# A state space mixer in chunks of 128 tokens with carried states, its preparation spread between the tiles of a branch projection

## The reference

```
c, L = s // CHUNK, CHUNK                                  # 4 chunks of 128 tokens
a_cs = jnp.cumsum(a, axis=2)                              # a = dt * A, within the chunk
decay = jnp.exp(jnp.where(causal, a_cs[l] - a_cs[s], -inf))
cb = jnp.einsum('bclgn,bcsgn->bclsg', cm, bm)
y_diag = jnp.einsum('bclsgr,bcsgrp->bclgrp', cb[..., None] * decay, xdt)
chunk_states = jnp.einsum('bclgn,bclgr,bclgrp->bcgrpn', bm, jnp.exp(a_cs[:, :, -1:] - a_cs), xdt)
state = state * chunk_decay + chunk_state                 # scan over the chunks, s_prev = state before
y_off = jnp.einsum('bclgn,bcgrpn,bclgr->bclgrp', cm, s_prev, jnp.exp(a_cs))
y = y_diag + y_off + xs * d_skip;  y = rmsnorm(y * silu(z))
```

## Time and profile before

| | |
|---|---|
| median of three runs (us) | 3278.84 |
| lowest and highest (us) | 3278.44, 3281.72 |
| span of the profiled execution (us) | 3281.5 |
| own time of the profiled execution (us), the run that goes with this span | 3281.72 |
| PE busy, share of the span | 97% |
| PEld, DVE, ACT, POOL busy | 77%, 56%, 28%, 11% |
| mean granted TensorE clock | 0.980 |

### The profile page before, as it was taken

The page is one execution under the profiler, slowest core; times in us unless marked ns, Lnnn a source line. Parts: engine busy times, 40 slices in busy tenths (PEclk is TensorE's granted clock), DMA queues, the critical chain, the costliest instruction groups (busy, mean ns, idle before and its releaser), DMA issues.

```text
span 3281.5 us, 37188 instructions
## 1 busy us (share of the span) xinstructions
PE 3186.0 (97%) x13833; PEld 2526.1 (77%) x13833; DVE 1850.9 (56%) x2389; ACT 923.5 (28%) x1243; POOL 346.3 (11%) x160
## 2 busy tenths in 40 slices
PE   8989999999999999999998999999999999999999
PEld 6767567877788887888877788887888887588887
DVE  8796435437776655554476755445454446465432
ACT  2443233323222222222222322222222234322222
POOL 2334014022000000000023000002000031000000
PEclk9999889999999999999999999999999998999999
DMA  3222002321323222223332222232223321022232
GB/s 129 78 77 90 26 32 90 116 77 61 119 91 99 96 97 91 90 96 99 102 107 77 77 96 96 97 103 95 96 96 99 105 76 46 7 97 90 96 105 88
DMA packets 79372, 287.67 MB, mean 88 GB/s; under 512 B 9056, under 2 KB 9312, under 8 KB 78880
## 3 DMA queue, kind: packets, MB, share of 16 engines
q1 hardware_dynamic: 77328, 278.03, 25.7%
q0 software_dynamic: 1936, 8.13, 0.7%
HBM read 284.02 MB, written 2.10 MB: 87 GB/s over the span
## 4 chain that ended last, share of the span: by engine, by line
PE 76%; issue 14%; POOL 5%; DVE 4%; ACT 1%; DMA 0%; POOLq 0%; DVEq 0%; ACTq 0%
PE ps L589 23%; PE ps L591 23%; PE ps L590 23%; POOL w_lo L543 5%; PE ps L682 1%; PE ps L1066 1%; PE ps L698 1%; PE ps L927 1%; PE ps L748 0%; PE ps L1065 0%; PE ps L1072 0%; DVE rstd L1566 0%; ACT w_hi L1110 0%; DVE w_lo L1502 0%; PE ps L933 0%
## 5 line engine op out<-in xcount | busy, mean ns | idle before, releaser
L589 PE MATMUL ps<-h_hi,w_hi 128*128 128x512 f32 (+1 forms) x2443 | 966.9, 396 | 33.8 <-POOL w_lo L543 20.8
L590 PE MATMUL ps<-h_lo,w_hi 128*128 128x512 f32 (+1 forms) x2443 | 956.4, 391 | 0.0
L591 PE MATMUL ps<-h_hi,w_lo 128*128 128x512 f32 (+1 forms) x2443 | 955.4, 391 | 0.0
L1110 ACT ACTIVATE w_hi<-raw 128x1024 fp32r<-128x1024 f32 x525 | 555.4, 1058 | 1315.6 <-PE ps L591 1297.8
L1502 DVE TENSOR_TENSOR w_lo<-raw,w_hi 128x1024 fp32r<-128x1024 f32 x390 | 476.9, 1223 | 450.3 <-ACT w_hi L1110 449.8
L589 PEld LDWEIGHTS ps<-h_hi,w_hi 128*128 128x128 f32 x2443 | 464.2, 190 | 142.8 <-POOL w_lo L543 24.6
L591 PEld LDWEIGHTS ps<-h_hi,w_lo 128*128 128x128 f32 x2443 | 464.0, 190 | 97.0
L590 PEld LDWEIGHTS ps<-h_lo,w_hi 128*128 128x128 f32 x2443 | 464.0, 190 | 96.5 <-issue 2.4
L589 PE MATMUL ps<-mid_hi,w_hi 128*128 128x512 f32 x1208 | 477.7, 395 | 2.0 <-DVE mid_lo L1577 2.0
L591 PE MATMUL ps<-mid_hi,w_lo 128*128 128x512 f32 x1208 | 476.9, 395 | 0.0
L590 PE MATMUL ps<-mid_lo,w_hi 128*128 128x512 f32 x1208 | 476.8, 395 | 0.0
(11 more groups left out here) (363 smaller groups left out, 2687.4 us busy)
## 6 DMA issues: line engine op xcount, KB each, us to landing
raw<-in_wstream SPq DMA_DIRECT2D x525, 512.0 KB, 3.3
x<-in_x SPq DMA_DIRECT2D x8, 256.0 KB, 5.6
x_in<-in_x POOLq DMA_DIRECT2D x8, 256.0 KB, 3.0
mem_x<-in_mem POOLq DMA_DIRECT2D x2, 1024.0 KB, 5.2
out<-x POOLq DMA_DIRECT2D x8, 256.0 KB, 3.5
tmp<-in_ret_decay POOLq DMA_DIRECT2D x1, 1024.0 KB, 5.2
rope_r<-in_rope_r POOLq DMA_DIRECT2D x1, 512.0 KB, 3.7
mats<-in_mats SPq DMA_DIRECT2D x1, 320.0 KB, 6.6
```

The costliest lines, as they stand in the source:

```text
L589: nc.tensor.matmul(dst, hi_w, hi_x, start=first, stop=False)
L590: nc.tensor.matmul(dst, hi_w, lo_x, start=False, stop=False)
L591: return nc.tensor.matmul(dst, lo_w, hi_x, start=False, stop=last)
L1110: nc.scalar.activation(w_hi[:, n % HL], raw[:, r], ACT.Copy).then_inc(hi_ready, 1)
```

## The change

It makes the mixer work as the reference does, chunk by chunk:

- A head has one `spread` over 512 columns (two matmuls, one bank, banks 4 and 5 by turns) and no mask by matmul. ACT takes the fall within the chunk with four `Relu` of 128 columns and then one `Exp` of 512; `cb` is now only the four diagonal blocks, multiplied by a 0/1 triangle in the preparation; DVE masks a head with one product of 512 (`masked`); PE makes four blocks of 128 columns (`y_diag`). `decay` has four slots in place of two.
- Six `chunk_state` matmuls of 512 columns, DVE's `weigh` and `carry`, and for each pair `y_carried` (three matmuls of 128 columns into bank 6) make the part that comes from earlier chunks. ACT makes `grown`, the exponential of the running sums (64 rows by 384 a head, two slots for pairs), and DVE's `pair_in` has three instructions in place of one.
- dt is multiplied into `xs_tok` when it is drained (four products of 128 columns in place of one copy for each of 8 tiles), no longer into `decay`.
- The preparation stands between the tiles of `br1`; the four scans (128 columns each, on 16 rows) stand ahead of the first product of `br1` on DVE; two of the eight gate tiles stand between the transposes of x, the other six one a pair in the loop.

```diff
+            br1_tiles(0, 2)
...
+            br1_tiles(2, 4)
...
+            br1_tiles(4, 6)
+            pe.wait_ge(aux_used, turned)
+            nc.tensor.matmul(aux_tile()[:, 0:64], IDENT[:, P - 1:P].to_broadcast([P, P]), acs_tok, start=True, stop=True)\
+                .then_inc(aux_done, 1)
+            br1_tiles(6, 8)
...
+            xs_turned(0, 4)
+            gate_tile(0)
+            xs_turned(4, 8)
+            gate_tile(1)
             pe.wait_ge(aux_used, aux[0])
+            pe.wait_ge(acs_ready, 2)
...
             def spread(hd):
+                if hd >= 2:
+                    pe.wait_ge(grown_done, hd - 1)
                 sel = ident_r[0:16, hd:hd + 1].to_broadcast([16, P])
-                for j, (b, cs) in enumerate(BANK_CHUNKS):
-                    if hd:
-                        pe.wait_ge(decay_done, 3 * hd - 2 + j)
-                    lo, hi = OFF[cs[0]], OFF[cs[-1]] + WIDTH[cs[-1]]
-                    dst = ps[:, b, 0:hi - lo]
-                    nc.tensor.matmul(dst, sel, acs_hi[:, lo:hi], start=True, stop=False)
-                    nc.tensor.matmul(dst, sel, acs_lo[:, lo:hi], start=False, stop=True)
-                    for c in cs:
-                        o = OFF[c] - lo
-                        mm = nc.tensor.matmul(dst[:, o:o + P], ident_r[:], neg_r[:, 0], start=False, stop=True,
-                                              skip_group_check=True)
-                mm.then_inc(bcast_done, 1)
-            spread(0)
-            for hd in range(SSD_HEADS):
-                if hd + 1 < SSD_HEADS:
-                    spread(hd + 1)
-                p = hd // 2
-                t, rows = st.t + 2 * p, slice(SSD_P * (hd % 2), SSD_P * (hd % 2) + SSD_P)
+                dst = ps[:, 4 + hd % 2]
+                nc.tensor.matmul(dst, sel, acs_hi[:], start=True, stop=False)
+                nc.tensor.matmul(dst, sel, acs_lo[:], start=False, stop=True).then_inc(bcast_done, 1)
+            def y_diag(hd):
+                t, rows, feats = y_tile(hd // 2), slice(SSD_P * (hd % 2), SSD_P * (hd % 2) + SSD_P), slice(SSD_P * hd, SSD_P * hd + SSD_P)
                 if hd % 2 == 0:
                     bank_free(t)
-                else:
-                    tile_part(st.n + p, t + 1, h_hi, h_lo, 0, 1, KB)
                 pe.wait_ge(m_ready, hd + 1)
                 for c in range(CH):
-                    mm = nc.tensor.matmul(bank(t)[rows, P * c:S], xs_tok[:, c, SSD_P * hd:SSD_P * hd + SSD_P],
-                                          decay[:, hd % 2, OFF[c]:OFF[c] + WIDTH[c]], start=c == 0, stop=True,
-                                          skip_group_check=c > 0)
+                    mm = nc.tensor.matmul(bank(t)[rows, P * c:P * c + P], xs_tok[:, c, feats],
+                                          decay[:, hd % 4, P * c:P * c + P], start=True, stop=True)
                 mm.then_inc(y_done, 1)
+            def chunk_state(g, c, b):
+                k = (CH - 1) * g + c
+                pe.wait_ge(weighed, g + 1)
+                if k >= 2:
+                    pe.wait_ge(state_taken, k - 1 if g == 0 else k)
+                nc.tensor.matmul(ps[:, b], b_tok[:, g, c], xw_tok[:, c, S * g:S * g + S], start=True, stop=True)\
+                    .then_inc(state_done, 1)
+            def y_carried(p):
+                g = p // 4
+                pe.wait_ge(state_taken, (CH - 1) * (g + 1))
+                if p:
+                    pe.wait_ge(posted, st.s + p)
+                for c in range(1, CH):
+                    mm = nc.tensor.matmul(ps[:, 6, P * c:P * c + P], states[c - 1][g][:, P * (p % 4):P * (p % 4) + P],
+                                          xbc[:, 10 + g, P * c:P * c + P], start=True, stop=True)
+                mm.then_inc(carried, 1)
+            spread(0)
+            spread(1)
+            chunk_state(0, 0, 6)
+            chunk_state(0, 1, 7)
+            for p in range(DT):
+                if p + 1 < DT:
+                    spread(2 * p + 2)
+                y_diag(2 * p)
+                if p == 0:
+                    chunk_state(0, 2, 6)
+                if p + 2 < DT:
+                    gate_tile(p + 2)
+                if p + 1 < DT:
+                    spread(2 * p + 3)
+                y_diag(2 * p + 1)
+                if 1 <= p <= 3:
+                    chunk_state(1, p - 1, 7)
+                if p:
+                    y_carried(p - 1)
+            y_carried(DT - 1)
...
+            gate_out(0)
+            split(st.n + 2)
+            gate_out(1)
             for hd in range(SSD_HEADS):
                 act.wait_ge(bcast_done, hd + 1)
-                if hd >= 2:
-                    act.wait_ge(y_done, hd - 1)
-                for b, cs in BANK_CHUNKS:
-                    for c in cs:
-                        o = OFF[c] - OFF[cs[0]]
-                        ins = nc.scalar.activation(decay[:, hd % 2, OFF[c]:OFF[c] + WIDTH[c]], ps[:, b, o:o + WIDTH[c]],
-                                                   ACT.Exp, bias=small[:, 80 + 16 * c + hd:81 + 16 * c + hd])
-                    ins.then_inc(decay_done, 1)
-                if hd % 2:
-                    split(st.n + hd // 2 + 1)
-                elif hd:
+                if hd >= 4:
+                    act.wait_ge(y_done, hd - 3)
+                for c in range(CH):
+                    ins = nc.scalar.activation(decay[:, hd % 4, P * c:P * c + P], ps[:, 4 + hd % 2, P * c:P * c + P], ACT.Relu,
+                                               bias=acs_tok[:, 16 * c + hd:16 * c + hd + 1], scale=-1.0)
+                ins.then_inc(fall_ready, 1)
+                act.wait_ge(fall_ready, hd + 1)
+                nc.scalar.activation(decay[:, hd % 4], decay[:, hd % 4], ACT.Exp, scale=-1.0).then_inc(decay_done, 1)
+                p, rows = hd // 2, slice(SSD_P * (hd % 2), SSD_P * (hd % 2) + SSD_P)
+                if p >= 2:
+                    act.wait_ge(posted, st.s + p - 1)
+                nc.scalar.activation(grown[rows, p % 2, P:S], ps[rows, 4 + hd % 2, P:S], ACT.Exp).then_inc(grown_done, 1)
+                if hd % 2 and hd // 2 < DT - 2:
+                    split(st.n + hd // 2 + 3)
+                elif hd % 2 == 0 and hd:
                     pair_out(hd // 2 - 1)
             pair_out(SSD_HEADS // 2 - 1)
...
             def pair_in(p):
-                drained_tile(st.t + 2 * p)
-                v.scalar_tensor_tensor(out=xbc[:, p], in0=xbc[:, p], scalar=vcol("ssd_d", p), in1=stage[:, (st.s + p) % 2],
-                                       op0=ALU.mult, op1=ALU.add).then_inc(posted, 1)
-            for hd in range(SSD_HEADS):
-                dve.wait_ge(decay_done, 3 * hd + 3)
-                g = hd * SSD_GROUPS // SSD_HEADS
-                for c in range(CH):
-                    rows = slice(OFF[c], OFF[c] + WIDTH[c])
-                    ins = v.scalar_tensor_tensor(out=decay[:, hd % 2, rows], in0=decay[:, hd % 2, rows],
-                                                 scalar=small[:, 16 + 16 * c + hd:17 + 16 * c + hd], in1=cb[:, g, rows],
-                                                 op0=ALU.mult, op1=ALU.mult)
-                ins.then_inc(m_ready, 1)
-                if hd and hd % 2 == 0:
-                    pair_in(hd // 2 - 1)
-            pair_in(SSD_HEADS // 2 - 1)
+                y, late = xbc[:, p], grown[:, p % 2, P:S]
+                dve.wait_ge(carried, p + 1)
+                dve.wait_ge(grown_done, 2 * p + 2)
+                done(v.tensor_tensor(late, late, ps[:, 6, P:S], ALU.mult))
+                drained_tile(st.t + (2 + 2 * p if p < DT - 2 else DT + p))
+                done(v.scalar_tensor_tensor(out=y, in0=y, scalar=vcol("ssd_d", p), in1=stage[:, (st.s + p) % 2],
+                                            op0=ALU.mult, op1=ALU.add))
+                v.tensor_tensor(y[:, P:S], y[:, P:S], late, ALU.add).then_inc(posted, 1)
+            def masked(hd):
+                dve.wait_ge(decay_done, hd + 1)
+                v.tensor_tensor(decay[:, hd % 4], decay[:, hd % 4], cb[:, hd * SSD_GROUPS // SSD_HEADS], ALU.mult)\
+                    .then_inc(m_ready, 1)
+            weigh(0)
+            masked(0)
+            carry(0, 0, 6)
+            carry(0, 1, 7)
+            masked(1)
+            carry(0, 2, 6)
+            weigh(1)
+            for hd in range(2, SSD_HEADS):
+                masked(hd)
+                if hd % 2 == 0 and hd >= 4:
+                    if hd <= 8:
+                        carry(1, hd // 2 - 2, 7)
+                    pair_in(hd // 2 - 2)
+            pair_in(DT - 2)
+            pair_in(DT - 1)
```

More of the change, by code:

```diff
@@ L346, in build @@
         u_hi, u_lo = br_hi, br_lo
+        acs = acc[0:SSD_HEADS]
+        dt_tok, acs_tok, tail, whole_chunk = (tok[:, k] for k in range(4))
+        states = [[tmp[:, 0], tmp[:, 1]], [tmp[:, 2], tmp[:, 3]], [spare[:, 0], spare[:, 1]]]
         x_squares = [tmp[:, k] for k in range(4)] + [stage[:, k] for k in range(2)] + [acc[:], spare[:, 0]]
@@ new lines, in _, with y_tile, gate_tile, xs_turned @@
```

(48 more changed lines are left out.)

119 lines of the change are left out of this document (73 added, 46 removed).

## The result

The changed kernel takes 3252.18 us (median of 4 runs, 3249.47 to 3254.73) beside 3280.28 for the kernel before on the same chip (4 runs, 3278.44 to 3286.96): 28.1 less by the medians. The ratio of all runs is 0.9909, its 95% interval 0.9896 to 0.9922. The profiled execution took 3254.7 with a span of 3252.9, against a span of 3281.5 before: 28.6 less. The forecast was 30.3 less, and 3249.

A forecast was written before the change was run, and what follows sets the result against it. PE's list of work was taken to bound the kernel. Loop 47.8 us less, 46.3 less with the preparation, minus 16 of clock loss: 30.3 less than the profiled or median time, said as 3249; range 3235 to 3267.

The forecast's parts named there:

- Preparation: From br1's first matmul to the loop: 66.1 us on PE, 1.5 more than before, with two gate tiles done in it.
- Prices on PE: Full-clock PE times in the loop: spread 0.66, four blocks 0.92, gate tile 5.67, carried part 0.69; an iteration 9.5 us.
- The ring: PE's spread waits for `grown`, that for `posted`, `pair_in` for `carried`: five pauses of 2.8 to 3.6 us, 15.6 together.
- The end of the loop: After the last gate tile, heads 13 to 15 and the last carried parts, without cover for ACT: 16.0 us at full clock.
- One sign that was to show the forecast wrong: In the loop, PE waiting for `m_ready`, that is for ACT's Relu or Exp.
- The clock: In the loop, 2.7 us lost at each of five pauses and the end: 16, ends 0 and 32.
- The sum: Whole kernel: 46.3 less at full clock, minus 16 of clock loss, 30.3 us less.
- its sign: For the loop's start: it begins within 2 us of 346.5.
- Rival 1: In the loop, each iteration's pause keeps the clock at 1.2 GHz throughout: 69 us more, 3301; chance 5%.
- Rival 2: In the loop, no pauses, `posted` earlier or the wait hidden: 15.6 less and half the clock loss, 3225; chance 9%.
- Rival 3: In the loop, POOL's panel work slows DVE's six `pair_in` by 2.1 us each: 12.6 more, 3261; chance 18%.
- the count of the prediction: In the loop, POOL's 2.45 us starts some 4.5 us into the iteration and ends ahead of `pair_in`.

The follow-up runs named there:

- e_prep: Changed kernel with its preparation put back in single stretches: all br1 tiles first, gate tiles 0 and 1 last; 3261.75 us, ratio 0.9934 to the kernel before.
- e_both: Changed kernel with a third `grown` slot, and `y_carried` and `chunk_state` ahead of the gate tile; 3219.84 us, in another session 3216.58.
- e_slots: Changed kernel with a third slot for `grown`, so ACT waits for the result of pair p-3; 3222.59 us, ratio 0.9829 to the kernel before.
- e_early: Changed kernel with `y_carried` and `chunk_state` moved ahead of the gate tile on PE, both slots kept; 3222.06 us, ratio 0.9829 to the kernel before.
- e_fill: Changed kernel plus 11 unread 128x512 matmuls after the carried part of iterations 1 to 5; 3244.48 us, ratio 0.9896 to the kernel before.
- e_zc: Changed kernel with third `grown` slot, carried part ahead of gate tile, and z's tiles 0 and 1 inside iterations 6 and 7; 3221.66 us.

## Why the prediction was right, point by point

- **Preparation**: forecast 66.1, measured 64.7 beside 64.6 before, so 1.4 less than forecast. PE has no wait there but one of 1.73 for the first panel. The small matmuls between the tiles took 6.4, forecast 7.7 with the 0.5 for a wait that didn't come. DVE's drains of x, forecast 9, took 6.6. e_prep shows what the covers are worth.
- **Prices on PE**: `spread` and blocks came nearly as read (at full clock 380.68 to 381.33 is 0.65 and 381.33 to 382.35 is 1.02, forecast 0.66 and 0.92). The first iteration took 9.9 (forecast 9.7), that of p = 1 10.8 (10.4); e_both's 9.66 stands against 9.5. Each block of 128 columns costs a little more than a quarter of 512.
- **The ring**: place, releaser, number and size as forecast: 14.0 us against 15.6. L1945, L1947 and L1949 have means of 0.55, 0.75 without one outlier, and 0.56 against 0.58, 0.75 and 0.58. `carry` added 0.66 where 0.8 was said. Two edits that open the ring at different places, e_slots and e_early, confirm the mechanism.
- **The end of the loop**: 21.84 from the spread at 434.14 to z, forecast 16.0 and a clock share of 2.7. One collision with POOL is in it, below. What is left, 21.84 - 16.0 - 1.65 = 4.2, is the clock, if the 16.0 was right; no run measures that number at full clock without another change. One sign that was to show the forecast wrong did appear here: PE waits for a head's mask (L1953) for 4.26 us. It is the one wait of that kind that the 16.0 had counted in, for head 15, and no iteration before has it.
- **The clock**: forecast 16 for six places, 2.7 each. Against e_slots' iteration of 10.74 and e_both's 9.66 the iterations from 370.20 lost 3.2, 3.2, 3.4 and 1.9, and with the end's 4.2 that is 15.9. The sum is right and its reason was not; that is luck. The loss of before was taken over, 21 us for eight pairs. But a third of the low clock stood in a stretch that hadn't begun in the loop. The kernel before stood in its preparation for 5.22 us ahead of 339.81, the clock fell at 338.7 in that wait and stayed low until 359.2, far into the loop (columns as in the earlier trace rows):

```profile
334.60:339.80 5.20, 0.00 (x0) 0.00 (x0) 5.03 (x8) 0.00 (x0) 0.00 (x0) 0.90 0.00 0
338.80:345.00 6.20, 4.63 (x24) 4.20 (x24) 5.70 (x11) 0.00 (x0) 0.00 (x0) 0.50 0.00 0
345.00:359.20 14.20, 13.35 (x28) 6.82 (x28) 4.40 (x7) 4.51 (x9) 1.47 (x1) 0.50 0.01 1
359.20:487.30 128.10, 128.10 (x454) 79.61 (x453) 48.82 (x65) 39.13 (x77) 18.67 (x8) 0.89 0.10 33
```

  So 14.2 of the 41.5 us of low clock belong to a stretch that began in a wait, and the other 27.3, behind 359.2, came with PE never idle. Whether the first stretch stayed low so long by the wait or by the thin work behind it, no run shows. After the change the loss comes with the pauses, since without them it is nearly gone. What I priced from thin matmuls was in the changed kernel a cost of the waits among them.
- **The sum**: 176.7 from br1 to z where it was 206.9, 30.2 less, forecast 30.3. That they agree to 0.1 is luck too: 1.4 less in the preparation and 1.6 less in the pauses stand against 1.65 more for the collision with POOL and 1.6 more for the work of the six iterations. Behind z's start the changed kernel needs 2796.9 where it was 2794.2: z's first tile runs partly at 1.2 GHz until 459.3, the last low stretch of the loop reaching over. Br1 started 1.1 earlier. Hence 28.6 in the span; the forecast had nothing for z. The loop began at 343.96, 2.5 before the 346.5 of the prediction, half a us outside its sign.

**The rivals.** Rival 1 (low clock throughout, 3301) fell: 41.1 of 112.0 us of the loop were low. The rule of the Trainium skill beside it, TensorE: Matmul & The Clock Gate, section Why this matters for your kernels, holds here as a direction: idle gaps between bursts brought half rate, and e_slots, e_early and e_fill, which take the gaps away in three ways, show it. It does not reach over a whole iteration: the gate tiles behind the pauses came back to full clock. Rival 2 (no pauses, 3225) fell, but the kernels without pauses, at 3222, came within 3 us of its price, though it kept 8 us of clock loss where e_slots has 1.2 us of low clock in its whole loop. Rival 3 (POOL inside the ring) happened once among seven, in the last `pair_in` but one:

```profile
451.57 2.40 DVE L1947 SCALAR_TENSOR_TENSOR xbc<-xbc,vec,stage 128x512 f32<-128x512 f32 x1
```

```profile
451.08 2.34 POOL L555 TENSOR_TENSOR w_lo<-raw,w_hi 128x1024 fp32r<-128x1024 f32 x1 [24.35 <-ACT w_hi L1176]
```

It costs 2.40 - 0.75 = 1.65, not 2.1, and in the five iterations POOL was through in time, as the count of the prediction had it. The same collision is in e_slots (above) and, behind z's start, in e_early and e_both.

On the fixed cost of short pieces (the Trainium skill, VectorE: DVE Perf Modes, section The TRN2 errata) the trace has four Relu in 1.11 us at 388.14, where the prediction had 1.14 from rows and, as an estimate by the page's table, 1.0. These Relu read PSUM, so of that section it is the table's row for PSUM that bears on them, not the advice for sources in SBUF. PE doesn't wait for them outside the loop's end.

## What to carry to other kernels

When work is cut into a ring over several engines, look at which instruction of PE stands last ahead of the ring's start, and put the long independent tile between the two: here one reordering of two calls was worth as much as a third buffer, and each as much as the whole change had given. A short wait on PE that comes back in every iteration is to be priced together with the clock behind it, here as much again. Before a clock loss is carried over to another kernel, look at where each low stretch begins: a third of the low time used here stood in a stretch that had begun in a wait of the stage before. After a wait is removed look at the next stage's first tile: in e_zc the whole gain had moved there, and one rounding issued earlier brought it back.

## What the runs showed that I had not expected

The clock gave back nearly all of its loss, not half. With no pause in the way, a thin part of 5.1 us between two gate tiles (e_slots, from the spread at 375.98 to the next gate tile at 381.05 in its timeline: spreads on 16 rows, blocks of 128x64, the carried part) left the clock at 2.4 GHz; with a pause of 2.54 to 3.20 in them it fell for 3.4 or 6.8 us each time. The length of a wait alone doesn't decide it: e_fill's clock fell behind one of 1.40, e_slots' stayed through one of 1.53. Nor is idle time the only thing that lowers it: the kernel before had 27.3 us of low clock from 359.2 to z with no idle time at all. What in its longer thin parts did that was not tried, and stays open.

A low stretch also reaches past the work that it began in, into the next stage: in the changed kernel the last one runs from 445.6 to 459.3, 3.3 us into z, whose first matmuls start 0.43 apart where later ones start 0.23 apart; in the kernel before the one of the preparation reaches 14.2 us into the loop.
